# Expert weights in eight slots, in loops over blocks of four experts, with 16 KB runs and the down bias added at the end

## The reference

```python
logits = (hf @ w_router) + b_router
top_v, top_i = lax.top_k(logits, TOP_K)        # 4 of 32 experts for each token
top_w = jax.nn.softmax(top_v, axis=-1)
...
def expert_block(args):
    xb, e = args
    gu = xb @ w_gate_up[e] + b_gate_up[e]       # [1024, 2048]
    gate = jnp.minimum(gu[:, :D_EXPERT], SWIGLU_LIMIT)
    up = jnp.clip(gu[:, D_EXPERT:], -SWIGLU_LIMIT, SWIGLU_LIMIT)
    glu = gate * jax.nn.sigmoid(SWIGLU_ALPHA * gate)
    return ((up + 1.0) * glu) @ w_down[e] + b_down[e]    # [1024, 1024]
```

## Time and profile before

| | |
|---|---|
| median of three runs | 1983.05 us |
| the profiled execution | 1978.14 us |
| its span, first to last instruction | 1976.0 us |
| outside the span | 2.14 us |
| TensorE busy (matmuls) | 1860.6 us, 94% |
| VectorE, ScalarE busy | 717.5 us and 544.5 us |
| moved by DMA | 587.06 MB, 297 GB/s over the span |
| mean granted TensorE clock | 0.975 |

### The profile page before, as it was taken

How to read it: one execution, slowest core, us unless ns; L and a number is a source line. 1 busy time by engine, 2 the same in 40 slices (tenths; PEclk the granted TensorE clock), 3 DMA queues, 4 the chain that set the end, 5 groups by cost and what they waited for, 6 DMA issues and landing times.

```text
span 1976.0 us, 25297 instructions
## 1 busy us (share of the span) xinstructions
PE 1860.6 (94%) x10316; PEld 1128.1 (57%) x10316; DVE 717.5 (36%) x1163; ACT 544.5 (28%) x714; POOL 34.3 (2%) x21
## 2 busy tenths in 40 slices
PE   6998989999999999999999999986799999889997
PEld 5775765344344343343443443374589987668996
DVE  3252232111111111111111111168765569565645
ACT  4352441111111111111111111144534444444342
POOL 0101010000000000000000000000000000000001
PEclk9999998999999999999999999996899999999999
DMA  9848669999999999999999999941045554314451
GB/s 330 311 160 339 228 237 410 418 419 417 418 418 417 419 418 417 419 417 417 419 417 418 418 417 418 416 165 43 31 161 179 203 192 168 131 65 170 182 205 39
DMA packets 136742, 587.06 MB, mean 297 GB/s; under 512 B 6462, under 2 KB 6676, under 8 KB 102900
## 3 DMA queue, kind: packets, MB, share of 16 engines
q1 hardware_dynamic: 135252, 581.25, 74.4%
q10 hardware_dynamic: 1440, 5.11, 0.7%
HBM read 585.29 MB, written 1.05 MB: 297 GB/s over the span
## 4 chain that ended last, share of the span: by engine, by line
PE 52%; DMA 38%; DVE 6%; ACT 2%; issue 1%; SPq 0%; DVEq 0%; ACTq 0%
DMA ring<-in_w_gate_up 35%; PE bank L1053 33%; PE bank L1305 9%; PE bank L1329 2%; DMA ring<-in_ada_w 1%; PE bank L1128 1%; PE bank L1265 1%; DMA ring<-in_ab_w_in 1%; PE bank L1432 1%; DVE sb_XN L2017 1%; PE bank L1338 1%; DVE sb_XN L2046 1%; PE bank L1113 1%; DMA ring<-in_w_o 1%; DVE sb_att L2021 0%
## 5 line engine op out<-in xcount | busy, mean ns | idle before, releaser
L1305 PE MATMUL bank<-ring,arena 128*64 128x512 f32 x2048 | 461.2, 598 | 14.1 <-DMA ring<-in_w_gate_up 14.1
L1305 PEld LDWEIGHTS bank<-ring,arena 128*64 128x64 f32 x2048 | 139.3, 137 | 329.8 <-issue 291.6
L1053 PE MATMUL bank<-w_hi,arena_r 128*128 128x512 f32 (+1 forms) x784 | 258.1, 391 | 4.7 <-DVE arena_r L2005 2.8
L1329 PE MATMUL bank<-ring,arena 128*64 128x512 f32 x1024 | 226.8, 595 | 0.0
L496 DVE TENSOR_TENSOR w_lo<-ring,w_hi 128x4096 fp32r<-128x4096 f32 (+2 forms) x45 | 196.5, 4367 | 54.1 <-ACT w_hi L486 51.7
L486 ACT ACTIVATE w_hi<-ring 128x4096 fp32r<-128x4096 f32 (+2 forms) x45 | 159.0, 3574 | 43.2 <-DMA ring<-in_c_w_in 20.4
L800 ACT ACTIVATE arena<-arena,sb_tab 128x512 f32<-128x512 f32 x32 | 23.1, 723 | 530.8 <-DVE arena L1910 530.8
L1053 PEld LDWEIGHTS bank<-w_hi,arena_r 128*128 128x128 f32 x784 | 148.0, 189 | 35.5 <-DVE arena_r L2005 3.3
L1884 DVE TENSOR_SCALAR arena<-sb_tab,sb_pos 128x64 f32<-128x64 f32 x66 | 13.8, 252 | 398.8 <-PE bank L1305 398.8
L1329 PEld LDWEIGHTS bank<-ring,arena 128*64 128x64 f32 x1024 | 70.7, 137 | 153.9 <-issue 153.9
L1910 DVE TENSOR_SCALAR arena<-bank 128x512 f32<-128x512 f32 x32 | 22.1, 692 | 360.0 <-PE bank L1305 360.0
(11 more groups left out here) (331 smaller groups left out, 2221.8 us busy)
## 6 DMA issues: line engine op xcount, KB each, us to landing
ring<-in_w_gate_up SPq DMA_DIRECT2D x128, 2048.0 KB, 24.4
ring<-in_w_down SPq DMA_DIRECT2D x64, 2048.0 KB, 22.4
ring<-in_mlp_w SPq DMA_DIRECT2D x32, 2048.0 KB, 8.3
ring<-in_ada_w SPq DMA_DIRECT2D x24, 2048.0 KB, 10.8
ring<-in_c_w_in SPq DMA_DIRECT2D x6, 2048.0 KB, 7.8
ring<-in_w_in SPq DMA_DIRECT2D x4, 2048.0 KB, 10.0
ring<-in_w_k SPq DMA_DIRECT2D x2, 2048.0 KB, 12.2
ring<-in_w_v SPq DMA_DIRECT2D x2, 2048.0 KB, 9.3
```

Source lines behind the costliest of these rows:

```text
L1053: mm = pe.matmul(out, st[a], mv[b], start=start and a + b == 0, stop=stop and a == 1, skip_group_check=True)
L1305: mm = pe.matmul(B[m][CAP * h:CAP * h + CAP, :], xe[:, 2 * j + kl, :], w[:, kl, m * D + h * HW:m * D + (h + 1) * HW], start=False, stop=(j ...
L1329: mm = pe.matmul(B[2][CAP * h:CAP * h + CAP, :], hT[:, c, CAP * j:CAP * j + CAP], w[:, c, h * HW:(h + 1) * HW], start=False, stop=(j == 1 ...
```

## The change

Eight slots serve the experts in place of six (`R1 = 8`): slots 6, 7, 4 and 5 ahead of the four of `PRE`. Since 24 granules, four experts, go evenly into eight slots, the loops of SP and PE have four experts in their body (`E_BLOCK = 4`); those of ACT and DVE stay at one. The first four expert granules are issued ahead of the end of `PRE` (`AHEAD`): two behind `ada` 18, when cross attention is through with slots 6 and 7, and two behind `ada` 20, when `w_o` is used up. `ada_part` moves to the arena.

In a granule, partition p now holds neighbouring rows, two of gate/up or four of down, which is one run of 16 KB. The rows of the stationary operands follow: `gather` reads every second element of `XN`, and `hidden_T` every fourth of the hidden rows. The gains of the norm are loaded again in that order (`ffn_gain`).

The down bias is no longer added for each expert. `bias_d` and `selD` go; the gates are transposed once (`gatT`), and behind the loop four matmuls add gates times `b_down` to the accumulators. `hidden_T` now stands ahead of `weights_T`, ACT copies them in that order, and PE waits for the copy of `weights_T` only behind `down`. The rarely used loop for experts with more than 64 tokens gets the same edits; it doesn't run on these inputs.

```diff
 R0 = 4
-R1 = 6
-E_SLOTS = [4, 5] + [(NPRE - R0 + j) % R0 for j in range(R0)]
+R1 = 8
+E_SLOTS = [6, 7, 4, 5] + [(NPRE - R0 + j) % R0 for j in range(R0)]
+E_BLOCK = 4
+AHEAD = {("ada", 18): (0, 1), ("ada", 20): (2, 3)}
 SPLIT = [p for p in PRE if p[0] != "ada"]
 PER_E = 6
 MOE_END = NPRE + NE * PER_E
...
 R2 = 4
-POST_SLOTS = [6, 7] + E_SLOTS[0:2]
-HI_SLOTS = E_SLOTS[2:6]
-X_SLOTS = E_SLOTS[0:2] + E_SLOTS[4:6]
+POST_SLOTS = E_SLOTS[0:4]
+HI_SLOTS = E_SLOTS[4:8]
...
         dft = ext[:, 4096:5120].rearrange("p (t n) -> p t n", t=TB)
-        ada_part = ext[:, 5120:6144].rearrange("p (i n) -> p i n", i=2)
+        ada_part = arn(9216, 1024).rearrange("p (i n) -> p i n", i=2)
         QT = ext[:, 6144:8192].rearrange("p (k s) -> p k s", k=KC)
         CT = arn(0, 1024)
...
+            def expert_source(j, e):
+                if j < 4:
+                    return A["w_gate_up"][0, bass.ds(e, 1), 2 * P * j:2 * P * (j + 1), :].rearrange(
+                        "e (p k) n -> p (e k n)", p=P)
+                return A["w_down"][0, bass.ds(e, 1), 4 * P * (j - 4):4 * P * (j - 3), :].rearrange(
+                    "e (p k) n -> p (e k n)", p=P)
+
+            def expert_fill(q, e):
+                s = slot_of(NPRE + q)
+                sp.dma_start(slot(s), expert_source(q % PER_E, e)).then_inc(landed[s], 16)
+
             for g, (name, i) in enumerate(PRE):
                 fill(g, name, i)
+                for q in AHEAD.get((name, i), ()):
+                    if q < 2:
+                        sp.wait_ge(sem("xa_o"), 4)
+                    else:
+                        sp.wait_ge(*done("w_o", 1))
+                    expert_fill(q, 0)
...
+                    sp.dma_start(ffn_gain[:].rearrange("p (j k) -> p j k", k=2),
+                                 A["norm_ffn"][0].rearrange("(j p k) -> p j k", p=P, k=2)).then_inc(sem("gain_landed"), 16)
...
-            for j in range(PER_E):
-                if OWNER[NPRE + j] is None:
-                    sp.wait_ge(*done("w_o", 1))
-                else:
-                    sp.wait_ge(used, USED_AT[OWNER[NPRE + j]])
-                s = expert_slot(j)
-                sp.dma_start(slot(s).rearrange("p (k n) -> p k n", k=2 if j < 4 else 4),
-                             expert_source(j, 0)).then_inc(landed[s], 16)
-            with sp.Fori(1, NE) as e:
-                for j in range(PER_E):
-                    s = expert_slot(j)
-                    sp.wait_ge(used, e * PER_E + (NPRE + j + 1 - PER_E))
-                    sp.dma_start(slot(s).rearrange("p (k n) -> p k n", k=2 if j < 4 else 4),
-                                 expert_source(j, e)).then_inc(landed[s], 16)
-
+            for q in range(4, R1):
+                sp.wait_ge(used, USED_AT[OWNER[NPRE + q]])
+                expert_fill(q, q // PER_E)
+            for q in range(R1, E_BLOCK * PER_E):
+                sp.wait_ge(used, NPRE + q - R1 + 1)
+                expert_fill(q, q // PER_E)
+            with sp.Fori(1, NE // E_BLOCK) as i:
+                for q in range(E_BLOCK * PER_E):
+                    sp.wait_ge(used, i * (E_BLOCK * PER_E) + (NPRE + q - R1 + 1))
+                    expert_fill(q, i * E_BLOCK + q // PER_E)
...
 
                 act.wait_ge(sem("e_clamp"), 2 * i + 1)
                 act.activation(sig, gcl, ACT.Sigmoid, bias=zero, scale=1.702).then_inc(sem("e_sig"), 1)
+                act.wait_ge(sem("e_hT"), i + 1)
+                act.activation(hT, B[0][:].rearrange("p (c n) -> p c n", c=4), ACT.Copy).then_inc(sem("e_hTe"), 1)
                 act.wait_ge(sem("e_wT"), i + 1)
                 act.activation(wselT, B[1][:, 0:TB * P].rearrange("p (t n) -> p t n", t=TB),
                                ACT.Copy).then_inc(sem("e_wTe"), 1)
-                act.wait_ge(sem("e_hT"), i + 1)
-                act.activation(hT, B[0][:].rearrange("p (c n) -> p c n", c=4), ACT.Copy).then_inc(sem("e_hTe"), 1)
                 if ahead is not None:
                     split_hi(act, *ahead)
...
                 for k in range(KC):
                     for t in range(TB):
-                        mm = pe.matmul(B[3][:, k * CAP:(k + 1) * CAP], XN[:, t, k * P:(k + 1) * P], sel_tok[:, t, :],
+                        rows = XN[:, t, 2 * P * (k // 2):2 * P * (k // 2 + 1)].rearrange("p (q r) -> p r q", r=2)
+                        mm = pe.matmul(B[3][:, k * CAP:(k + 1) * CAP], rows[:, k % 2, :], sel_tok[:, t, :],
                                        start=(t == 0), stop=(t == 1))
                 mm.then_inc(sem("e_gather"), 1)
...
+            for t in range(TB):
+                mm = pe.transpose(B[6][0:NE, t * P:(t + 1) * P], gat[:, 0:NE, t], ident)
+            mm.then_inc(sem("gat_T"), 1)
...
                 for c in range(4):
-                    mm = pe.transpose(B[0][:, c * P:(c + 1) * P], hh_[:, c * P:(c + 1) * P], ident)
+                    mm = pe.transpose(B[0][:, c * P:(c + 1) * P], hh_.rearrange("p (q c) -> p c q", c=4)[:, c, :], ident)
                 mm.then_inc(sem("e_hT"), 1)
-
-            def bias_d():
-                for h in range(2):
-                    pe.matmul(B[2][CAP * h:CAP * h + CAP, :], selD[0:NE, :], bias_dn[:, h * HW:(h + 1) * HW],
-                              start=True, stop=False)
 
             def down(j, s):
                 w = slot(s).rearrange("p (k n) -> p k n", k=4)
                 for c in range(4):
                     for h in range(2):
                         mm = pe.matmul(B[2][CAP * h:CAP * h + CAP, :], hT[:, c, CAP * j:CAP * j + CAP],
-                                       w[:, c, h * HW:(h + 1) * HW], start=False, stop=(j == 1 and c == 3))
+                                       w[:, c, h * HW:(h + 1) * HW], start=(j == 0 and c == 0),
+                                       stop=(j == 1 and c == 3))
                 return mm
...
-            with pe.Fori(0, NE) as i:
-                pe.wait_ge(sem("e_selG"), i + 1)
-                pe.wait_ge(sem("e_xe"), i + 1)
+            def expert(i, n):
+
+                pe.wait_ge(sem("e_selG"), i * E_BLOCK + (n + 1))
+                pe.wait_ge(sem("e_xe"), i * E_BLOCK + (n + 1))
                 bias_gu()
                 for j in range(4):
-                    g = NPRE + j
-                    pe.wait_ge(landed[slot_of(g)], i * 16 + FILL[g])
+                    g = NPRE + n * PER_E + j
+                    pe.wait_ge(landed[slot_of(g)], i * (16 * E_BLOCK * PER_E // R1) + FILL[g])
                     gate_up(j, slot_of(g)).then_inc(used, 1)
                     if j == 0:
-                        pe.wait_ge(sem("acc_zero"), 4)
-                        pe.wait_ge(sem("e_y"), i + 1)
+                        pe.wait_ge(sem("acc_zero"), 5)
+                        pe.wait_ge(sem("e_y"), i * E_BLOCK + (n + 1))
                         scatter()
-                pe.wait_ge(sem("e_sel"), 2 * i + 4)
+                pe.wait_ge(sem("e_sel"), i * (2 * E_BLOCK) + (2 * n + 4))
                 gather()
-                pe.wait_ge(sem("e_wsel"), 2 * i + 2)
-                pe.wait_ge(sem("e_clamp"), 2 * i + 2)
+                pe.wait_ge(sem("e_h"), i * E_BLOCK + (n + 1))
+                hidden_T()
+                pe.wait_ge(sem("e_wsel"), i * (2 * E_BLOCK) + (2 * n + 2))
+                pe.wait_ge(sem("e_clamp"), i * (2 * E_BLOCK) + (2 * n + 2))
                 weights_T()
-                pe.wait_ge(sem("e_h"), i + 1)
-                hidden_T()
-                pe.wait_ge(sem("e_selD"), i + 1)
-                bias_d()
-                pe.wait_ge(sem("e_wTe"), i + 1)
-                pe.wait_ge(sem("e_hTe"), i + 1)
+                pe.wait_ge(sem("e_hTe"), i * E_BLOCK + (n + 1))
                 for j in range(2):
-                    g = NPRE + 4 + j
-                    pe.wait_ge(landed[slot_of(g)], i * 16 + FILL[g])
+                    g = NPRE + n * PER_E + 4 + j
+                    pe.wait_ge(landed[slot_of(g)], i * (16 * E_BLOCK * PER_E // R1) + FILL[g])
                     down(j, slot_of(g)).then_inc(used, 1)
+                pe.wait_ge(sem("e_wTe"), i * E_BLOCK + (n + 1))
+
+            with pe.Fori(0, NE // E_BLOCK) as i:
+                for n in range(E_BLOCK):
+                    expert(i, n)
+            for t in range(TB):
+                for h in range(2):
+                    pe.matmul(B[4 + 2 * t + h][:], gatT[:, t, :], bias_dn[:, h * HW:(h + 1) * HW], start=False, stop=False,
+                              skip_group_check=True)
...
             def gains_xe():
-                g = VEC["norm_ffn"]
-                dve.tensor_tensor(xe, B[3][:].rearrange("p (k n) -> p k n", k=KC), bc(col[:, g:g + KC], CAP),
+                dve.tensor_tensor(xe, B[3][:].rearrange("p (k n) -> p k n", k=KC), bc(ffn_gain[:], CAP),
                                   ALU.mult).then_inc(sem("e_xe"), 1)
 
...
             dve.wait_ge(sem("ada_done"), len(ADA_READS))
+            dve.wait_ge(sem("gat_T"), 1)
```

(14 more changed lines are left out.)

14 lines of the change are left out of this document (4 added, 10 removed).

## The result

The changed kernel takes 1961.4 us in the median of four runs (1954.93 to 1969.38), the kernel before 1984.49 (four runs beside it): ratio 0.989, interval 0.9867 to 0.9913. That is 23 us less where 30 were forecast. A second set of runs gave 1961.29 and 0.9903 (0.9882 to 0.9924), 22 us less. Against the 1953 forecast the time lies inside the range of 1943 to 1975 and 1.4 us above the 1945 to 1960 of case A.

What follows compares the result with a forecast made beforehand. The prediction took DMA to bound the loop, with PE 0.75 us per expert behind. Loop 28.3 plus tail 2.6 minus small edits 0.5 gave 30.4 us less: 1953 against a median of 1983.05, range 1943 to 1975.

Steps and rivals of the forecast that it cites:

- case A: Whole kernel: the forecast itself holds, 1945 to 1960 us, chance 0.48.
- What bounds it: Expert loop: DMA sets the pace now, PE 0.75 us per expert behind; after the change PE sets it.
- E: Weight supply: 16 KB runs bring nothing, 1966 us, chance 0.07; below 411 GB/s, 1981 us, chance 0.04.
- PE's sequence: Expert loop on PE: 0.40 us less per expert, 28.97 us each, loop ending 28.3 us earlier.
- B: hidden_T: transposes slower from reads in 16-byte steps, 0.44 us more per expert, 1967 us, chance 0.24.
- D: gather: its 32 loads per expert take twice as long, 3.7 us per expert, 2072 us, chance 0.07.
- The copy takes the place of the bias: Ahead of down: the 1.23 us removed aren't all gained, because bias_d covered ACT's copy of hidden_T.
- The 0.40: Ahead of down: saving taken per expert in us, between bounds of 0.23 and 0.50.
- The start: Ahead of the loop: the second pair of early fills delays ada 21 to 23, loop begins 4.5 us later.
- The end: Behind the loop: 2.6 us less for the tail, the bias matmuls' 1.92 us hidden.
- ACT's part: Behind the loop: ACT splits the second piece of ab_in 0.6 us after down instead of 3.2, 2.6 us less.
- C: Expert loop: longer body fetched again at each of 7 jumps back, 14 to 34 us, middle 1977, chance 0.10.

Runs made afterwards that it cites:

- runs_only: Kernel before with only the expert weights in 16 KB runs and matching reads and gain columns; six slots, no early fills, bias_d in every expert: 1970.70 us.
- bias_back: Changed kernel with bias_d back in every expert, between weights_T and down, without the four bias matmuls at the end: 1974.78 us.
- gap_filled: Changed kernel with the last of gather's eight column groups (two matmuls) issued behind hidden_T instead of ahead of it: 1949.96 us.
- gateup_8k: Changed kernel with gate/up alone in the old order (8 KB runs, contiguous reads in gather), down still in 16 KB runs: 1960.35 us.

## Why the forecast was right in kind and 7 to 9 us too large

- **What bounds it: right.** DMA leaves the chain, PE sets the pace of all 32 experts. The supply was better than forecast, 428 GB/s for 426, and E falls. The last expert weights were no bound: PE never waits for any.
- **PE's sequence: right but for the reads.** "So 28.97 us for each expert": with contiguous reads it is 28.96. The step that failed is that `gather` and `hidden_T` keep their durations. B and D, which I priced as doublings (0.44 and 3.7 us per expert), both came true in small: 0.07 and 0.20 us, together 0.27, 8.3 us over 31 experts. The period of 29.23 so lies above the 28.9 to 29.1 that the prediction named, and below its 29.3. "The bytes in B speak against it" compared bytes per ns with `down`'s moving operands; a load of a stationary operand in steps isn't priced by those.
- **The copy takes the place of the bias: right.** It leaves 0.74 us between `hidden_T` and `down` in the chain, and filling it gave 0.47 per expert. The 0.40, chosen between 0.23 and 0.50, came out by 0.01 with contiguous reads, in part by luck: the gap is 0.67 to 0.74 us where 0.83 follows from the forecast, and `down` takes 0.07 more.
- **The start: right in mechanism and, over many executions, in size.** The pair delays `ada`, PE waits 3.1 us in one profile and 3.6 in the other, and the start is 1.4 to 7.5 us longer than the 59.5 before. Between the means with and without the pair lie 4.5 us, and 4.5 was forecast; with starts that fall at 61 or 67, so close a match of means is in part luck. I hadn't seen that the clock behind the wait makes two sizes of it.
- **The end: wrong.** ACT's part held (13.45 us without the bias matmuls). The step that failed is "the four bias matmuls take as long as a scatter, 1.92 us". `scatter`'s matmuls lie in two groups of rows and run in pairs; the bias matmuls all read the same 32 rows and run one after the other, 3.63 us. They are on the path, and the keep-busy matmuls and a lower clock come behind them: 3.1 to 4.4 us more than without bias matmuls, and 1.4 where the clock stayed at 1.00.
- **C falls in the loop and shows behind it.** In 335 to 1250 us of the first profile the instruction queue moved this, and the only waits of PE are those for the copy:

```profile
q8 instruction: 4, 0.07, 0.0%
```

```profile
PE bank L1334 <- ACT arena L808: 16.8, 32, 0.5
```

Four pieces of 16 KB in the first pass, none at a jump back, and each of the seven jumps back takes 0.22 to 0.23 us. The Trainium skill, Advanced Engine Details and Errata, ISA Cache, gives TensorE 128 KB, and 256 instructions for 16 KB, so room for 2048, an estimate from the page; four experts are some 1230 matmuls and loads. The trace agrees.

What I hadn't looked for is PE's one branch behind the loop, past the code for experts with more than 64 tokens. Before, and in the second profile of the changed kernel:

```profile
L1375 PEldq COMPARE_BRANCH  x1: 348/348/348, 1285.3 to 1285.3; - x1
```

```profile
L1388 PEldq COMPARE_BRANCH  x1: 3404/3404/3404, 1259.3 to 1259.3; - x1
```

In all eleven profiles with the bias matmuls behind the loop it takes 3.2 to 5.9 us, and a 16 KB instruction piece moves while it lasts; in the kernel before, runs_only and bias_back it takes 0.35 to 0.46 us, and none does. That the branch waits for the piece is likely from this, not tested. In the changed kernel it ends 2 us or more before `scatter` does and costs nothing; with a shorter or later PE it cost 0.8 to 4.2 us, as above.

**Open** is what makes the clock fall at one place or another of the start and the end. It isn't the wait alone. In the first profile of the changed kernel it was 0.57 for the 10.7 us behind the wait of 3.1 us and 0.69 for the 10.9 after them; in the second one `ada` unit behind the wait of 2.8 us was slow (3.28 us), and then, from 311.6 on, it was 1.00. It also fell in profiles without any such wait, the kernel before among them (0.75 from 306.6 to 320.4). With the same code it moves a single execution by 6 us at the start (61 or 67) and by 1.3 at the end (16.5 or 17.8), as much as an experiment on them could bring. Open too is why the shorter loops of gap_filled and gateup_8k bring 3 to 5 us less in the median than in the loop.

## What to carry to other kernels

When a stage is bound by its supply and the next bound is close behind, work out that one's own sequence: here eight slots in place of six, and the early fills, changed the loop by 0.6 us each or less once runs of 16 KB had put DMA 0.1 us per expert behind PE, and the next 0.5 us came from moving two matmuls into a wait. A layout that makes DMA's runs longer changes the step of somebody's reads; time the whole group of such loads before counting it as free. And a matmul's price depends on which rows its neighbours use: take it from a row with the same placement, not the same size.

## What was not expected of the hardware

- Runs of 16 KB move 428 to 429 GB/s, against 418 for the mix of 8 and 4 KB.
- In the mean, a load of a 128x128 stationary operand took 192 ns contiguous and 196 in steps of 8 bytes; one by transposes 155 and 219 ns in steps of 16 bytes. The Trainium skill, Advanced Engine Details and Errata, SBUF Cachelines, would let the first go free and make the second pay. The trace agrees by the single load, at 2% and 41%, but not by the group: the 32 loads in steps of 8 bytes lengthened `gather` by 0.20 us, and the four in steps of 16 bytes `hidden_T` by 0.07.
- Float32 matmuls of 32 rows overlap when they lie in different groups of rows: four of them (eight instructions of 512 columns) took 1.92 us in two groups, and 3.63 in one.
- One branch of PE took 0.35 us in the kernel before and 3.2 to 5.9 us in eleven others, each time with a 16 KB instruction piece under way.
